# Index queries projected feature by feature, six down-projection units, index scores by row halves in turn, in a three-layer fp32 kernel

## The reference, cut to what matters

```python
def _shared_latent_kv(x, w_down, kv_norm, w_up):
    c = x @ w_down                                  # 512 latent + 64 rotary columns
    lat = _rms_norm(c[..., :KV_LORA], kv_norm)
    k_rope = _rope(c[..., KV_LORA:], ROPE_BASE_B)
    ...
def _mla_layer(x, w_in, q_norm, ...):
    hproj = x @ w_in                                # 768 query-latent columns, then the gate
    ...
def hybrid_layer(x, norm1_w, w_in, ...):
    h = rms_norm(x, norm1_w)
    u = h @ w_in
    rnn_x, rnn_gate, q, k, v, iq, ik, iw, g = jnp.split(u, offsets, axis=-1)
    ...
    ik = rms_norm(ik, idx_k_norm_w)
    y_attn = dsa_attention(q, k, v, iq, ik, iw)     # the 64 best keys of each query
    ...
# in dsa_attention, for eight index heads of 64 features
rel = relu(einsum('bqhd,bsd->bqhs', iqc, ik))
score = einsum('bqhs,bqh->bqs', rel, iwc) * idx_scale
```

## Time and profile before

| what | value |
|---|---|
| median of three runs | 874.88 us (873.28 to 874.88) |
| profiled execution, its own time | 874.96 us |
| its span, first to last instruction | 873.6 us |
| TensorE busy | 868.7 us, 99% |
| TensorE weight loads | 781.2 us, 89% |
| VectorE busy | 602.5 us, 69% |
| ScalarE busy | 489.2 us, 56% |
| GpSimd busy | 101.5 us, 12% |
| DMA | 154.31 MB, mean 177 GB/s |
| chain that ended last | TensorE 98%, DMA 1% |

### The profile page before, as it was taken

One profiled execution on the slowest core, in us unless ns is written; L12 is line 12 of the kernel. 1 busy time (PEld: TensorE's weight loads), 2 busy tenths in 40 slices (PEclk: granted clock), 3 DMA queues, 4 the chain that ended last, 5 costly groups with the idle time before them and its releaser, 6 DMA issues.

```text
span 873.6 us, 13512 instructions
## 1 busy us (share of the span) xinstructions
PE 868.7 (99%) x5621; PEld 781.2 (89%) x5621; DVE 602.5 (69%) x886; ACT 489.2 (56%) x686; POOL 101.5 (12%) x50
## 2 busy tenths in 40 slices
PE   8999999999999999999999999999999999999998
PEld 7898898888999999999888899999999888888887
DVE  5976666559687777778478888878966676664442
ACT  6555445433656666665428677997744565553330
POOL 0110101000000000000000000224000045551000
PEclk9999999999999999999999999999999999999999
DMA  9844554642563444455465444233445555555520
GB/s 344 327 161 183 193 203 173 231 149 83 204 215 132 156 154 156 156 198 188 176 239 194 192 162 177 97 117 125 146 154 218 208 192 190 185 183 198 195 86 24
DMA packets 25117, 154.31 MB, mean 177 GB/s; under 512 B 3168, under 2 KB 3808, under 8 KB 8928
## 3 DMA queue, kind: packets, MB, share of 16 engines
q1 hardware_dynamic: 23312, 148.97, 47.3%
q10 hardware_dynamic: 1584, 3.96, 1.3%
q0 software_dynamic: 160, 0.52, 0.2%
HBM read 152.39 MB, written 1.05 MB: 176 GB/s over the span
## 4 chain that ended last, share of the span: by engine, by line
PE 98%; DMA 1%; SPq 0%; ACT 0%; issue 0%; DVE 0%; ACTq 0%
PE ps L414 26%; PE ps L416 25%; PE ps L415 25%; PE ps L505 6%; PE ps L508 3%; DMA a_first<-in_k_part 1%; PE ps L558 1%; PE ps L521 1%; PE ps L559 1%; PE ps L741 1%; PE ps L565 1%; PE ps L904 1%; PE ps L932 1%; PE ps L637 1%; PE ps L751 1%; PE ps L921 1%
## 5 line engine op out<-in xcount | busy, mean ns | idle before, releaser
L1591 DVE TENSOR_TENSOR w_lo_ring<-w_raw,w_hi_ring 128x2048 fp32r<-128x2048 f32 (+3 forms) x145 | 312.8, 2167 | 141.2 <-ACT w_hi_ring L1109 140.9
L1109 ACT ACTIVATE w_hi_ring<-w_raw 128x2048 fp32r<-128x2048 f32 (+3 forms) x145 | 260.9, 1808 | 111.3 <-PE ps L416 105.4
L414 PE MATMUL ps<-xT_hi,w_hi_ring 128*128 128x256 f32 x488 | 138.9, 285 | 0.0
L415 PE MATMUL ps<-xT_lo,w_hi_ring 128*128 128x256 f32 x488 | 136.7, 280 | 0.0
L416 PE MATMUL ps<-xT_hi,w_lo_ring 128*128 128x256 f32 x488 | 136.5, 280 | 0.0
L414 PEld LDWEIGHTS ps<-xT_hi,w_hi_ring 128*128 128x128 f32 x488 | 92.1, 189 | 1.6 <-issue 0.8
L414 PE MATMUL ps<-w_hi_ring,xT_hi 128*128 128x512 f32 (+1 forms) x240 | 92.5, 385 | 0.0
L415 PEld LDWEIGHTS ps<-xT_lo,w_hi_ring 128*128 128x128 f32 x488 | 92.2, 189 | 0.2
L416 PEld LDWEIGHTS ps<-xT_hi,w_lo_ring 128*128 128x128 f32 x488 | 92.1, 189 | 0.0
L416 PE MATMUL ps<-w_hi_ring,xT_lo 128*128 128x512 f32 (+1 forms) x240 | 91.8, 382 | 0.0
L415 PE MATMUL ps<-w_lo_ring,xT_hi 128*128 128x512 f32 (+1 forms) x240 | 91.7, 382 | 0.0
(11 more groups left out here) (360 smaller groups left out, 1812.2 us busy)
## 6 DMA issues: line engine op xcount, KB each, us to landing
w_raw<-in_a_w_in SPq DMA_DIRECT2D x21, 1024.0 KB, 4.9
w_raw<-in_w_ff_in SPq DMA_DIRECT2D x16, 1024.0 KB, 4.8
w_raw<-in_w_ff_out SPq DMA_DIRECT2D x16, 1024.0 KB, 4.7
w_raw<-in_b_w_uq SPq DMA_DIRECT2D x16, 576.0 KB, 4.2
w_raw<-in_a_w_out SPq DMA_DIRECT2D x8, 1024.0 KB, 4.8
w_raw<-in_b_w_gate SPq DMA_DIRECT2D x8, 1024.0 KB, 4.7
w_raw<-in_kv_w_up SPq DMA_DIRECT2D x8, 1024.0 KB, 4.8
w_raw<-in_b_w_out SPq DMA_DIRECT2D x8, 1024.0 KB, 5.2
```

The source lines that it names most:

```text
L414: k.T.matmul(out, lh, rh, start=start, stop=False, skip_group_check=True)
L415: k.T.matmul(out, lh, rl, start=False, stop=False, skip_group_check=True)
L1109: k.A.activation(k.hi[:, in_slot(u)], k.raw[u % RING][:, 0:size(u)], ACT.Copy).then_inc(k.s["w_hi"], 1)
L1591: k.V.tensor_tensor(k.lo[:, in_slot(u)], k.raw[u % RING][:, 0:size(u)], k.hi[:, in_slot(u)].bitcast(F32), ALU.subtract).then_inc(k.s["w_lo ...
```

## The change

Three things are edited.

1. The down projections have six units and not eight: the rest of the query latents is one unit of 2048 columns, the rotary keys one of 1024.
2. The units `QKVI` lose iq and are six, `QKV`. The index keys are multiplied behind the fifth unit and turned right away; the two halves of the scaled input are turned behind the fifth and the sixth. The index queries follow as two feature-major units `U_IQ` from the scaled input, into PSUM banks 4 and 5, and ScalarE copies each straight to `c_iqT` (`act_index_queries`). The turns of iq are gone. The exponential and the twenty small VectorE instructions of `dve_softplus8` move behind the normalisation of the heads.
3. `pe_index_scores` takes four heads in one call, in the order `BOTH_SIDES` that the attention scores already had, and asks for all four banks before its first matmul.

```diff
-U_QKVI, U_RNNX, U_MAIN, ... = 80, 88, 92, 108, 112, 116, 132, 148
+U_QKV, U_IQ, U_RNNX, U_MAIN, ... = 78, 84, 86, 90, 106, 110, 114, 130, 146
...
+BOTH_SIDES = ((0, 0), (1, 1), (2, 0), (3, 1), (0, 1), (1, 0), (2, 1), (3, 0))
...
 def pe_index_scores(k, i, hd):
-    bank, rows = pe_small_bank(k, i), half_rows(hd)
-    for q, cols in enumerate(QCOLS):
-        m = k.T.matmul(bank[:, cols], k.c_iqT[rows, hd // 2, q * P:(q + 1) * P], k.c_ikT[rows, 0:(q + 1) * P],
-                       start=q == 0, stop=True, skip_group_check=True)
-    m.then_inc(k.s["small_mm"], 1)
+    banks = [pe_small_bank(k, i + r) for r in range(4)]
+    for turn, (r, q) in enumerate(BOTH_SIDES):
+        rows = half_rows(r)
+        m = k.T.matmul(banks[r][:, QCOLS[q]], k.c_iqT[rows, (hd + r) // 2, q * P:(q + 1) * P], k.c_ikT[rows, 0:(q + 1) * P],
+                       start=turn < 4, stop=True, skip_group_check=True)
+        if turn >= 4:
+            m.then_inc(k.s["small_mm"], 1)
...
 def pe_hybrid(k):
-        if b >= 2 and half == 0:
-            T.wait_ge(s["c_drain_a"], b - 1)
-            T.wait_ge(s["c_drain_v"], b - 1)
-        if n == 6:
-            pe_index_keys(k)
-        token_major(k, U_QKVI + n, ...)
-        if b == 3:
+        if n == 4:
+            T.wait_ge(s["c_drain_a"], 1)
+            T.wait_ge(s["c_drain_v"], 1)
+        token_major(k, U_QKV + n, ...)
+        if b == 2:
+            if half == 0:
+                pe_index_keys(k)
+            else:
+                T.wait_ge(s["c_drain_a"], 2)
+                T.wait_ge(s["c_drain_v"], 2)
             T.wait_ge(s["c_h0"], half + 1)
             T.wait_ge(s["c_h1"], half + 1)
-            if half == 1:
-                T.wait_ge(s["c_ikw"], 1)
             for c in range(2):
                 pe_turn_pair(k, "hs", 2 * half + c, ...)
             if half == 0:
                 pe_turn_index_keys(k)
 
+    T.wait_ge(s["c_ikw"], 1)
+    for n in range(2):
+        feature_major(k, U_IQ + n, k.xT, KD, S, halves(ps[:, 4 + n, :]), ("turned_lo", TURN["hs"]) if n == 0 else None)
...
-            pe_to_features(k, 0, "iq", 0)
-            pe_to_features(k, 1, "iq", 2)
             pe_to_features(k, 2, "q", 0)
             pe_to_features(k, 3, "q", 2)
...
+    act_hi(k, U_IQ + AHEAD)
+    A.wait_ge(s["c_drain_a"], 3)
     A.wait_ge(s["c_drain_v"], 3)
     A.wait_ge(s["c_ikw"], 1)
...
     act_root(k, ROOT["heads"], ...)
+    act_index_queries(k, 0)
+    act_hi(k, U_IQ + 1 + AHEAD)
+    A.wait_ge(s["c_sp_in"], 1)
+    A.activation(k.c_lam[1], k.c_lam[1], ACT.Exp).then_inc(s["c_sp_exp"], 1)
+    act_index_queries(k, 1)
```

More of the change, by code:

```diff
@@ L363, in sp_program @@
     load(k, U_QLAT + 2, d["b_w_qlat"][0, 1])
-    for n in range(2):
-        load(k, U_QREST + n, d["b_w_qrest"][0, n])
+    load(k, U_QREST, d["b_w_qrest"])
     load(k, U_LATENT, d["kv_w_down"][0, 1])
-    for n in range(2):
-        load(k, U_KROPE + n, d["kv_w_rope"][0, n])
+    load(k, U_KROPE, d["kv_w_rope"])
     for pair in range(HB // 2):
@@ L375, in sp_program @@
     sp_output(k, U_BOUT, d["b_w_out"])
-    for n in range(8):
-        load(k, U_QKVI + n, d["w_qkvi"][QKVI[n]])
+    for n, part in enumerate(QKV):
+        load(k, U_QKV + n, d["w_qkv"][part])
+    for n in range(2):
+        load(k, U_IQ + n, d["w_iq"][n])
     for n in range(8):
@@ L703, in pe_latents @@
     T.wait_ge(s["turned_lo"], TURN["a"] + 4)
[L704 to L710, removed]
-    token_major(k, U_LATENT, k.xT, 4, 4, 512, [ps[:, 2 + t, :] for t in range(NT)], False, True)
[L712 to L716, removed]
+    wh, wl = weights(k, U_QREST, KD, S)
+    for n in range(KD):
+        for t in range(NT):
+            x = tuple(z[:, n, t * P:(t + 1) * P] for z in k.xT)
+            m = mm3(k, ps[:, 4, t * S:(t + 1) * S], x, (wh[:, n, :], wl[:, n, :]), n == t == 0, n == KD - 1)
+    m.then_inc(s["w_used"], 1)
+    token_major(k, U_LATENT, k.xT, 4, 4, 512, [ps[:, 2 + t, :] for t in range(NT)], False, True)
+    wh, wl = weights(k, U_KROPE, KD, P)
+    for n in range(KD):
+        m = mm3(k, ps[:, 6, 0:S], (wh[:, n, :], wl[:, n, :]), tuple(z[:, n, :] for z in k.xT), n == 0, n == KD - 1)
+    m.then_inc(s["w_used"], 1)
     T.wait_ge(s["b_qlat"], 1)
@@ L1011, in pe_hybrid @@
             T.wait_ge(s["small_read"], 7)
-            for hd in range(4):
-                pe_index_scores(k, 8 + hd, hd)
+            pe_index_scores(k, 8, 0)
         elif n == 1:
-            for hd in range(4, IH):
-                pe_index_scores(k, 8 + hd, hd)
+            pe_index_scores(k, 12, 4)
         elif n in (2, 3):
@@ L1245, in act_latents @@
         A.activation(k.b_junk[:, t, :], ps[:, t, :], ACT.Square, accum_out=k.b_sq[:, t, 0:1])
-    for n in range(3, 5):
-        act_hi(k, U_QLAT + n + AHEAD)
+    act_hi(k, U_QLAT + 3 + AHEAD)
     A.wait_ge(s["w_used"], U_LATENT)
@@ L1396, in act_hybrid @@
             m = A.activation(k.c_qk[:, 0, b * 512:(b + 1) * 512], bank, ACT.Copy, scale=root)
-        elif b == 2:
+        else:
             A.activation(k.c_qk[:, 0, D:D + 256], bank[:, 0:256], ACT.Copy, scale=root)
             m = A.activation(k.c_v[:, 0, :], bank[:, 256:512], ACT.Copy, scale=root)
-        else:
-            m = A.activation(k.c_iq[:, 0, :], bank, ACT.Copy, scale=root)
         m.then_inc(s["c_drain_a"], 1)
@@ L1816, in dve_latents @@
     V.wait_ge(s["tablesB_in"], 16 * 4)
-    for n in range(5):
+    for n in range(4):
         dve_lo(k, U_QLAT + n + AHEAD)
@@ L1997, in dve_hybrid @@
     V.sem_inc(s["c_total"], 1)
-    for n in range(1, 8):
+    for n in range(1, 6):
         if n != 2:
-            dve_lo(k, U_QKVI + n + AHEAD)
+            dve_lo(k, U_QKV + n + AHEAD)
         if n == 1:
@@ L2356, in layout @@
     out["b_w_qlat"] = units(w[:, :512], 4, 512)
-    out["b_w_qrest"] = units(w[:, 512:QL], 4, S)
+    out["b_w_qrest"] = units(w[:, 512:QL], KD, S)[0, 0]
     out["b_w_gate"] = units(w[:, QL:], KD, 2 * VH)[:, 0]
```

105 lines of the change are left out of this document (49 added, 56 removed).

## The result

| | before | after |
|---|---|---|
| median of 13 runs, us | 874.84 (873.28 to 875.38) | 876.35 (875.64 to 876.68) |
| ratio | 1 | 1.0019, 95% interval 1.0011 to 1.0027 |
| profiled execution: own time, span | 874.96, 873.6 | 875.64, 874.3 |

What follows compares the result with a forecast made beforehand. TensorE, busy 868.7 of 873.6 us, was taken as the bound. Terms 0 + 0.33 - 0.87 + 1.41 + 0.65 - 0.11 = +1.41 us on 874.96 gave 876.4 us, range 874.4 to 877.7.

Steps and rivals of the forecast that it cites:

- Index keys, +1.41: Ahead of the index keys' product: TensorE waits for the weight's low part, signal and restart included, +1.41 us.
- Index scores, heads 0 to 3, +0.65: First group of index scores: all four banks asked for first, so it starts only after copies c_kT, +0.65 us.
- Index queries, +0.33: Index queries: two token-major units (10.88 us) give way to two feature-major units (11.21 us), +0.33 us.
- turns, -0.87: Turns of iq: a block of 16 turns (1.66 us) becomes one of 8 (0.79 us), -0.87 us.
- Heads 4 to 7, -0.11: Second group of index scores: runs at the attention scores' 1.50 us in place of 1.61, -0.11 us.
- Down projections, 0: Down projections in six units: same matmuls at 0.117 us each and no gap to win, 0 us.
- Sum: Whole kernel: all terms together +1.41 us, added to the profiled execution's 874.96 us, giving 876.4 us.
- The keys do wait: Answers the rival that the index keys don't wait: sum +0.0, 875.0 us; chance 10%.
- so does the first group: Answers the rival that neither the index keys nor heads 0 to 3 wait: -1.42, 873.5 us; chance 8%.
- The row halves do not run side by side: Answers the rival that both halves overlap in the index scores, 0.64 us less per group: 875.1 us; chance 5%.
- The handshake of the softplus: Rival: ScalarE falls behind by the third recurrent unit, delaying c_kT; 878.9 us if 5 us late, 876.9 if 3; chance 10%.
- Six units do not help: Answers the rival that six down-projection units free TensorE through a place in the ring: 872.5 us; chance 5%.

Runs made afterwards that it cites:

- Run 1: Changed kernel with the index keys' weight split earlier, high part on ScalarE and low part on VectorE; 874.66 us, ratio 1.0003 to the kernel before.
- run 2: Changed kernel with ScalarE's copies c_ikT and c_kT ahead of its split of the next weights; 874.46 us, ratio 1.0001 to the kernel before.
- run 4: Changed kernel with the index scores of before, head by head without alternating row halves; 875.72 us, ratio 1.0013 to the kernel before.
- run 5: Kernel before with only ScalarE's copies c_ikT and c_kT put ahead of its weight split; 873.92 us against 874.45, ratio 0.9993.
- run 8: Changed kernel with each of the four banks asked for only just before its first matmul; 875.58 us in one execution.

## Why the prediction was right, point by point

- **Index keys, +1.41.** Measured 1.29 of delay and 0.06 of slower restart, 1.35. That is 0.06 under the forecast. Run 1 took it away and got 1.4 us back.
- **Index scores, heads 0 to 3, +0.65.** From the last matmul ahead of the group to the end of the group it was 2.48 us (528.21 to 530.69) and is 3.24: +0.76. I had the copies' end right to 0.1 us against the unit's end; the restart behind the wait (530.02 to 530.16) was 0.09 longer than the 0.05 I gave it. Runs 2, 4, 5 and 8 show it from four sides.
- **Index queries, +0.33, and turns, -0.87.** The stretch from the index keys to the second recurrent unit is 29.16 against 28.38, and 1.35 of it is the wait: -0.57 against -0.54. Three feature-major units took 16.89, so two index units 11.20.
- **Heads 4 to 7, -0.11.** Measured 1.51 for 1.61, -0.10. The unit between the groups, which I had not named, is 0.06 shorter (5.58 against 5.64 from its first to its last start).
- **Down projections, 0.** Wrong by 0.15 us. "The same matmuls run" is so, but not at the same pace. It is small beside the rest, and a term of the sum that the form of the argument had ruled out. Nor was 0.117 us "the pace of any feature-major unit": in the trace of before, units of the first layer run at 0.120 (last section).
- **Sum.** -0.57 + 1.35 + 0.76 - 0.06 - 0.10 + 0.15 = +1.53, against +1.41 forecast and 1.51 between the medians. The two misses, 0.11 at the scores and 0.15 at the down projections, are made good in part by 0.06 at the keys, 0.03 at the queries and 0.06 in the unit between. So the nearness of 0.05 us is in part luck: the errors of the terms go both ways, and the forecast was added to the profiled execution (874.96 us), 0.12 above the median of before, which makes up for the 0.10 by which the sum was short. The measured difference is itself known only to about 0.7 us; what bears out the single terms is the profile. The profiled span came out at 874.3 and not near 875.0, since the wait on L467 was 0.8 us shorter in that execution. One slip: 0.3 less and 0.5 more is 876.1 to 876.9 us, not the "own range" of 875.9 to 877.1; no term hangs on it.
- **The rivals.** The keys do wait and so does the first group. The row halves do not run side by side: 1.51 us for 3072 columns in both groups, as in the earlier trace rows, so the rule of the Trainium skill's page "TensorEngine Tiling (Array Packing)", section "Tiling Modes", gave nothing for this pattern either. What taking the halves in turn gives is 0.10 us a group (1.61 head by head in run 4, 1.51 in turn); why, no run shows. The handshake of the softplus did not put ScalarE behind: ahead of `c_xc` it stood idle 2.51 us for TensorE, to the hundredth what it did before. Six units do not help.
- **What the forecast did not say:** that both waits could be had back by moving one or two instructions each, on engines with idle time. The rows on which the two terms rested already showed that idle time.

## What to carry to other kernels

When a change brings TensorE to an operand sooner, list who makes that operand and what stands ahead of it on its engine: here 2 us of squares and 1.9 us of weight splitting that nobody needed yet, and moving the operand's maker ahead of them turned a loss of 1.5 us into a gain of 1.0. When several banks or tiles are asked for together, the group starts with the latest of them, so a reordering that saves 0.1 us can cost 0.8. And a unit that is said to run "the same matmuls" is checked by its pace in the trace, also in a part of the program that seems untouched.

## What the runs showed that I had not expected

**A longer wait cost more than its length.** With a gap of 1.5 us from one matmul's start to the next the granted clock stayed at full speed in all 24 executions; with 2.4 us it fell in half of them, with 4.8 in all five, and in the profiled one of these the slower clock cost 2.7 us on top. The Trainium skill, page "TensorE: Matmul & The Clock Gate", section "What's actually happening", says that the gate knows two levels, 1.2 and 2.4 GHz, and goes down behind idle time; the trace agrees, with 0.50 in the product behind the wait. The waits of this change did not bring that about, but they were near to it: with the low part 0.8 us later the median rose by 1.8.

**256-column matmuls of one unit ran at 0.120 us each in place of 0.117.** The rest of the query latents took 5.75 us in all twelve profiles of kernels with six down-projection units (218.72 to 224.47 in the changed one) and 5.6 in the two with eight, the kernel before and run 5, for the same 48 matmuls with the same shapes. What differs is where the unit begins in its slot: 16 columns in before (64 bytes), 8 now (32 bytes). The trace of the kernel before has the same difference between other units. The two feature-major units of the second head of the first layer, whose weights begin 8 columns in, took 11.51 us for 96 matmuls, 0.120 each, from the first of these rows to the last:

```profile
43.34 0.28 PE L414 MATMUL ps<-xT_hi,w_hi_ring 128*128 128x256 f32 x1
...
54.85 1.03 PE L649 MATMUL ps<-ident,a_o 128*128 128x128 f32 x8
```

So did those of the third and the fourth head. The three units of 16.89 us further up have the same shapes and the same moving tile, with weights that begin at the slot's first column, and took 0.117. So the pace went with the unit's place, whether its weights move or stand still. No run changed the place and nothing else; that the place is the cause is likely and not shown. If it is, the six units of the first layer would give back 288 times 0.003, about 0.9 us (an estimate from these rows). Matmuls of 512 columns say nothing on it: the 24 of the next unit took 5.47 us in both kernels, and begin 8 columns in in both.
